# Weight buffers moved by multiples of 64 bytes against the stationary tiles of TensorE

## The chip, the cores and the metric

The kernel runs on one core of one Trainium2 chip. The metric is the device time of one execution in microseconds (us), from the program's start on the chip to its end.

## The reference

One layer of a decoder trunk, batch 1, 256 positions, 4096 channels, all in float32. A pre-RMSNorm is followed by four token mixers that share one input projection, and by a PEER channel mixer with 4096 experts:

```python
xn = rmsnorm(x, norm_mix)
cols = xn @ w_in                         # 256x4096 @ 4096x5200, split by mixer
o_a, o_b, o_c, o_d = four attention mixers of the columns
z = xn @ gate_down                       # 256 wide
merged = sum(sigmoid(z @ gate_up[i]) * (o_i @ w_branch_i) for i in range(4))
h = x + merged @ w_out                   # 4096x4096
hn = rmsnorm(h, norm_ffn)
q = hn @ peer_wq                         # 4096x1024, top-k keys and gates
out = h + (w * gelu(hn @ u.T)) @ v       # w: expert weights from the top keys
```

The weights are read once; with 256 rows, each weight tile serves two row tiles (h = 0, 1) of 128 positions.

## The kernel before, in words

**Products.** All large products run as one stream of 680 chunks. A chunk is 256 rows (two k-tiles, j = 0, 1) by up to 512 columns of weights. The activations are the stationary operand, the weights the moving one. To keep float32 accuracy with TensorE's float32r type, each operand is split in a hi and a lo part, and three products are added: hi x hi, lo x hi, hi x lo (activation x weight). One chunk is 12 matmuls: `products` (L551 on) issues 4 on L559 (activations hi, weights hi), 4 on L562 (activations lo, weights hi) and 4 on L566 (activations hi, weights lo), over j and h. `branch_products` does the same on L607, L609 and L613, `first_products` on L578, L582 and L586 for the first 16 chunks, which are 336 columns wide, `last_products` on L954 to L956 for the last chunk. The other 664 chunks are 512 columns wide: 664 x 12 = 7968 matmuls.

**Order.** The stages follow one another over the same stream: input projection (11 column groups of 16 chunks), gates and branches, output projection, PEER queries, `u` and `v`. Between chunks `between(s)` puts the small matmuls of the mixers, of the key search and of the expert scatter at slots written out by hand. Other matmuls and transposes use plain float32 or bfloat16.

**The ring.** Four slots (`RING`), each with three buffers in SBUF: `w_raw` (loaded by SP's DMA queue once `lo_ready` says that the slot's old content was split), `w_hi` (written by ACT, L979, a copy of `w_raw` into float32r, once `chunk_used` says that TensorE is done with the old chunk), and `w_lo` (DVE, L1340, `w_raw - w_hi`). TensorE waits for `hi_ready` before a chunk and for `lo_ready` before its last four matmuls. A slot's buffer is 4096 bytes in each partition: the tile of j = 0 at its start, the tile of j = 1 at `width` x 4 bytes, which is 2048 for 512 columns and 1344 for the first group's 336.

**Places.** A stationary tile is 128 columns x 4 bytes = 512 bytes in each partition. `xt_hi` and `xt_lo` begin at `XT0`, with 1024 bytes to a k-tile and h = 1 at +512; `ot_*` and `zt` are put on multiples of 512 bytes from `PJ0` by `over` (L221 on), `x2_*` begins at `PJ0` and `x3_*` at `XT0` plus whole KB. `PJ0` is a whole number of 512 bytes behind `XT0`. `w_raw`, `w_hi` and `w_lo` begin at `RG0`, at `RG0` + 16 KB and at `RG0` + 32 KB. So every 512-wide moving tile begins a whole number of 512 bytes from every stationary tile. In this document the distance of a moving tile is the remainder of that number by 512: it is 0 for all 512-wide ones, and in the first group 0 for j = 0 and 1344 - 1024 = 320 for j = 1.

**Small buffers that the diff touches.** `cmp_h` (hidden layer of the compressed keys, L709, L1054, L1450), `row_at` (a table of the key search, L1702 to L1724), `iota_h` (bfloat16 counting row, L1700, L1813, L1822), `small` (320 floats of per-row scalars, cut up by `piece`).

Of the kernel before, what the change touches and what calls it, by code (L numbers as in the profile page):

```python
# [19 lines left out]
F32R = mybir.dt.float32r  # L20
BF16 = mybir.dt.bfloat16
# [5 lines left out]
P = 128  # L27
# [39 lines left out]

RING = 4
LEAD = RING - 1
CPG = KT // 2  # L70
GRP = D // 512
MERGE = ("b", "c", "d", "a")
MIX_K = {"b": 4, "c": 4, "d": 2, "a": 4}
CH_MIX = NG1 * CPG
MIX_CH, _c = {}, CH_MIX
# [3 lines left out]
CH_OUT = _c  # L79
CH_WQ = CH_OUT + GRP * CPG  # L80
CH_U = CH_WQ + 2 * CPG
CH_V = CH_U + GRP * CPG
CH_END = CH_V + GRP * CPG

# [6 lines left out]
NCMP = (S - 32) // 16 + 1  # L91
PH, PK = 8, 16
KB = 1024
# [41 lines left out]
TURN_Q, COPY_Q, SCORE_K, COPY_K = 2, 6, 6, 10  # L135
RANK_AT = CH_WQ + CPG + COPY_K + 1
SOFTMAX_AT = RANK_AT + (NT * PH // UNITS) * STEPS
PICKS_TURN = SOFTMAX_AT + 1
SCATTER_AT = PICKS_TURN + LEAD + 2
ROUND_AT = {SCATTER_AT + n + n // 11: n for n in range(ROUNDS)}  # L140
PUT_END = max(ROUND_AT) + LEAD + 1
WEIGH_AT = {max(PUT_END + 2 + q, CH_V + CPG // 2 + 3 + q - 14 if q >= 14 else 0): q for q in range(CPG)}
# [30 lines left out]
def build(nc, io):  # L173
# [1 line left out]
    base = (nc.sbuf_base + 31) // 32 * 32  # L175
    XT0 = base
    RG0 = XT0 + 64 * KB
    MG0 = RG0 + 12 * RING * KB
    CN0 = MG0 + 32 * KB

    def at(name, shape, dt, off):
        return nc.alloc_sbuf_tensor_at(name, shape, dt, offset=off)

    cursor = [CN0]

    def const(name, shape, dt=F32):
        t = at(name, shape, dt, cursor[0])
        cursor[0] += (int(np.prod(shape[1:])) * 4 + 31) // 32 * 32
        assert cursor[0] <= nc.sbuf_usable_end, name
        return t  # L190
# [3 lines left out]
    xt_lo = at("xt_lo", [P, KT, S], F32R, XT0 + 32 * KB)  # L194

    w_raw = at("w_raw", [P, RING, 1024], F32, RG0)
    w_hi = at("w_hi", [P, RING, 1024], F32R, RG0 + 4 * RING * KB)
    w_lo = at("w_lo", [P, RING, 1024], F32R, RG0 + 8 * RING * KB)

    xt_raw = at("xt_raw", [P, KT, S], F32, MG0)  # L200
    rows = at("rows", [P, NT, D], F32, MG0)
    feat = {"c": at("feat_c", [P, 6, S], F32, MG0), "b": at("feat_b", [P, 7, S], F32, MG0 + 8 * KB),
            "d": at("feat_d", [P, 8, S], F32, MG0 + 8 * KB), "a": at("feat_a", [P, 8, S], F32, XT0),
            "i": at("idx_t", [P, 3, S], F32, MG0 + 16 * KB)}
    probs_of = [at(f"probs{h}", [P, 6, (h + 1) * P], F32, MG0 + 16 * KB) for h in range(NT)]
# [38 lines left out]
    pe_t = const("pe_t", [P, 2, 32])  # L244
    cmp_w2 = const("cmp_w2", [P, 2, P])
    cmp_b = const("cmp_b", [P, 2, 32, NCMP])
    cmp_h = const("cmp_h", [P, 2, NCMP])

    def cmp_at(i):

# [37 lines left out]
    pair_n = const("pair_n", [P, UNITS, PK], U32)  # L288
    pair_m = const("pair_m", [P, UNITS, PK], U32)
    pair_f = const("pair_f", [P, 2, UNITS, PK])  # L290
    row_at = const("row_at", [P, PK])
    fifteen = const("fifteen", [P, UNITS, PK], U32)
    iotas = const("iotas", [P, P])
    iota_h = const("iota_h", [P, P], BF16)

    square = at("square", [P, D], F32, XT0)
    peer_q = at("peer_q", [P, NT, PH * HD], F32, XT0)
# [26 lines left out]
    def piece(n, parts=P):  # L324
        used[0] += n
        return small[0:parts, used[0] - n:used[0]]
# [5 lines left out]
    row_max, row_neg, row_den, row_inv = piece(6), piece(6), piece(6), piece(6)  # L332
    nsa_gate, top8, k_ms, k_rstd = piece(24), piece(8), piece(1, NCMP), piece(1, NCMP)
    soft_den, soft_inv = piece(16), piece(16)


    acc = nc.alloc_psum_tensor("acc", [P, 2, NT, 512], F32)
# [100 lines left out]
    def mix_end(b, n):  # L438

        return MIX_CH[b] + (n + 1) * (1 + MIX_K[b] // 2) - 1  # L440


    MIX_OUT = {mix_end(b, n) + LEAD: (b, n) for b in MERGE for n in range(GRP)}
    GATE_OUT = {MIX_CH[b] + n * (1 + MIX_K[b] // 2) + LEAD: (b, n) for b in MERGE for n in range(GRP)}
    OUT_OUT = {CH_OUT + (n + 1) * CPG + LEAD: n for n in range(GRP)}

    MIX_BLOCK = {mix_end("a", n) + LEAD + 1: n for n in range(GRP)}
    MIX_STORE = {mix_end("a", n) + LEAD + 5 + i: (n, (2 * i, 2 * i + 1)) for n in range(GRP) for i in range(2)}
# [1656 lines left out]
```

How the kernel before makes its waits and increments, by code:

```python
        def then(instruction):  # L393
            count[0] += 1
            instruction.then_inc(own, 1)
            eng.wait_ge(own, count[0])
# [28 lines left out]
    def evacuated(eng, group):  # L425
        eng.wait_ge(bank_free[group % 2], group // 2 + 1)
        if group:
            eng.wait_ge(bank_free[(group - 1) % 2], (group - 1) // 2 + 1)
# [33 lines left out]
        @block.sync  # L463
# [1 line left out]
            def load(src, slot, width, used_by=None):  # L465
                if used_by is not None:
                    sp.wait_ge(lo_ready, used_by)
                sp.dma_start(w_raw[:, slot, 0:width], src).then_inc(raw_loaded[slot], 16)
# [12 lines left out]
            def load_in(chunk, g, slot, used_by=None):  # L481
                if used_by is not None:
                    sp.wait_ge(lo_ready, used_by)
                into = w_raw[:, slot, 0:2 * in_width(g)].rearrange("p (j n) -> p j n", j=2)
                end = FIRST + SKEW * g
                if g:
                    sp.dma_start(into[:, :, 0:512 - end], in_tile(chunk - CPG, slice(end - SKEW, W1C)))\
                        .then_inc(raw_loaded[slot], 16)
                sp.dma_start(into[:, :, in_width(g) - end:], in_tile(chunk, slice(0, end)))\
                    .then_inc(raw_loaded[slot], 16)
# [14 lines left out]
                        load_in(m * RING + c, g, c, m * RING + (c - RING + 1))  # L506
                if g == 6:
                    sp.wait_ge(cmp_hidden, 4)
                    sp.dma_start(dil[:], io["dil"]).then_inc(dil_loaded, 16)
```

## Time and profile before

| | us |
|---|---|
| median of the runs (2 runs, 1931.16 to 1931.26) | 1931.21 |
| the profiled execution | 1931.49 |
| its span, first to last instruction | 1929.3 |

The profiled execution lies 0.28 us above the median, and 2.2 us of it lie outside the span. In the profile, PE is the row of matmuls and PEld that of the loads of stationary tiles (LDWEIGHTS), which overlap the matmuls. The recorded length of a matmul (390 ns for 512 columns) includes its pipeline, so successive ones overlap. The pace of the stream is read from starts: the start of one group of 4 less that of the one before, over 4.

### The profile page before, as it was taken

To read this page: it belongs to the slowest core of one execution; us is meant where nothing else is said; L and a number is where in the kernel's file an instruction comes from. 1 tells how busy PE (TensorE), PEld (TensorE's weight loads), DVE (VectorE), ACT (ScalarE), POOL (GpSimd) and SP (SyncE) were. 2 spreads that over 40 slices of the span, in tenths; PEclk is the share of its full clock that TensorE was granted. 3 is DMA by queue.
4 is the path that set the end of the run, shared out by engine and by line. 5 is a ranking of instruction groups with operands and counts; after the bars stand their busy time and mean duration, and the time that the engine had idled before them with its cause. 6 is when DMAs were issued, how large, how long until landed. Compare 5 with 4: busy or idle time off the path is not lost.

```text
span 1929.3 us, 26583 instructions
## 1 busy us (share of the span) xinstructions
PE 1924.4 (100%) x9284; PEld 1588.5 (82%) x9284; DVE 1274.3 (66%) x1876; ACT 933.7 (48%) x1146; POOL 37.0 (2%) x50
## 2 busy tenths in 40 slices
PE   9999999999999999999999999999999999999999
PEld 8888888888888888888888888888887788888887
DVE  6578775675557889655555555788878876444444
ACT  6653644444566556444444464444444454333332
POOL 0010010000000000000000000000000000000000
PEclk9999999999999999999999999999999999999999
DMA  9976666566655669877777776667766578666664
GB/s 321 351 221 166 171 177 192 163 164 173 184 177 179 178 206 290 286 228 244 239 233 217 217 226 223 227 213 215 221 214 189 176 232 285 202 206 207 200 204 140
DMA packets 198537, 412.62 MB, mean 214 GB/s; under 512 B 45760, under 2 KB 123968, under 8 KB 197792
## 3 DMA queue, kind: packets, MB, share of 16 engines
q1 hardware_dynamic: 173616, 368.83, 62.9%
q10 hardware_dynamic: 20976, 25.19, 3.9%
q0 software_dynamic: 3840, 17.17, 2.4%
q8 instruction: 70, 1.15, 0.2%
q14 instruction: 35, 0.29, 0.0%
HBM read 390.15 MB, written 20.97 MB: 213 GB/s over the span
## 4 chain that ended last, share of the span: by engine, by line
PE 99%; DMA 0%; SPq 0%; ACT 0%; DVE 0%; issue 0%
PE acc L559 29%; PE acc L562 29%; PE acc L566 29%; PE acc L607 3%; PE acc L609 3%; PE acc L613 3%; PE side L737 1%; PE side L848 1%; PE acc L578 0%; PE acc L582 0%; PE acc L586 0%; PE side L772 0%; PE side L663 0%; DMA w_raw<-in_w_in 0%; PE side L748 0%; PE side L702 0%
## 5 line engine op out<-in xcount | busy, mean ns | idle before, releaser
L1340 DVE TENSOR_TENSOR w_lo<-w_raw,w_hi 128x1024 fp32r<-128x1024 f32 (+1 forms) x680 | 825.4, 1216 | 607.4 <-ACT w_hi L979 604.6
L979 ACT ACTIVATE w_hi<-w_raw 128x1024 fp32r<-128x1024 f32 (+1 forms) x680 | 715.0, 1053 | 817.8 <-PE acc L566 738.7
L559 PE MATMUL acc<-w_hi,xt_hi 128*128 128x512 f32 x1660 | 449.3, 393 | 0.0
L562 PE MATMUL acc<-w_hi,xt_lo 128*128 128x512 f32 x1660 | 444.4, 390 | 0.0
L566 PE MATMUL acc<-w_lo,xt_hi 128*128 128x512 f32 x1660 | 444.2, 390 | 0.0
L562 PEld LDWEIGHTS acc<-w_hi,xt_lo 128*128 128x128 f32 x1660 | 311.8, 188 | 65.2
L566 PEld LDWEIGHTS acc<-w_lo,xt_hi 128*128 128x128 f32 x1660 | 311.8, 188 | 64.9
L559 PEld LDWEIGHTS acc<-w_hi,xt_hi 128*128 128x128 f32 x1660 | 308.9, 188 | 63.4 <-issue 1.8
L559 PE MATMUL acc<-w_hi,x_hi 128*128 128x512 f32 x640 | 175.2, 396 | 0.0
L562 PE MATMUL acc<-w_hi,x_lo 128*128 128x512 f32 x640 | 171.9, 391 | 0.0
L566 PE MATMUL acc<-w_lo,x_hi 128*128 128x512 f32 x640 | 171.3, 390 | 0.0
L562 PEld LDWEIGHTS acc<-w_hi,x_lo 128*128 128x128 f32 x640 | 120.2, 188 | 25.6
L566 PEld LDWEIGHTS acc<-w_lo,x_hi 128*128 128x128 f32 x640 | 120.2, 188 | 25.3
L559 PEld LDWEIGHTS acc<-w_hi,x_hi 128*128 128x128 f32 x640 | 117.3, 188 | 22.4
L1121 ACT ACTIVATE gate<-acc 128x512 f32<-128x512 f32 x64 | 34.8, 596 | 35.1 <-PE acc L566 35.0
L559 PE MATMUL acc<-w_hi,zt_hi 128*128 128x512 f32 x128 | 34.5, 392 | 0.0
L566 PE MATMUL acc<-w_lo,zt_hi 128*128 128x512 f32 x128 | 34.3, 390 | 0.0
L562 PE MATMUL acc<-w_hi,zt_lo 128*128 128x512 f32 x128 | 34.3, 390 | 0.0
L1585 DVE TENSOR_TENSOR gate<-acc,gate 128x512 f32<-128x512 f32 x48 | 30.8, 683 | 0.0
L1063 ACT ACTIVATE probs<-probs,small 128x128 f32<-128x128 f32 (+2 forms) x44 | 18.3, 417 | 22.0 <-DVE small L1498 21.9
L562 PEld LDWEIGHTS acc<-w_hi,zt_lo 128*128 128x128 f32 x128 | 24.1, 188 | 5.0
L566 PEld LDWEIGHTS acc<-w_lo,zt_hi 128*128 128x128 f32 x128 | 24.0, 188 | 5.0
(279 smaller groups left out, 1345.4 us busy)
## 6 DMA issues: line engine op xcount, KB each, us to landing
w_raw<-in_stream SPq DMA_DIRECT2D x504, 512.0 KB, 4.2
w_raw<-in_w_in SPq DMA_DIRECT2D x16, 496.0 KB, 4.2
w_raw<-in_w_in SPq DMA_DIRECT2D x16, 480.0 KB, 4.0
w_raw<-in_w_in SPq DMA_DIRECT2D x16, 464.0 KB, 3.7
w_raw<-in_w_in SPq DMA_DIRECT2D x16, 448.0 KB, 3.8
w_raw<-in_w_in SPq DMA_DIRECT2D x16, 432.0 KB, 3.9
w_raw<-in_w_in SPq DMA_DIRECT2D x16, 416.0 KB, 3.9
w_raw<-in_w_in SPq DMA_DIRECT2D x16, 400.0 KB, 3.7
```

Source lines behind the costliest of these rows:

```text
L559: pe.matmul(o[h], lhs(k0 + j, h)[0], wh[j], start=first and j == 0, stop=False)
L562: pe.matmul(o[h], lhs(k0 + j, h)[1], wh[j], start=False, stop=False)
L566: mm = pe.matmul(o[h], lhs(k0 + j, h)[0], wl[j], start=False, stop=last and j == 1)
L607: pe.matmul(o, lhs(k0 + j, h)[0], wh[j], start=first and j == 0, stop=False)
L609: pe.matmul(o, lhs(k0 + j, h)[1], wh[j], start=False, stop=False)
L613: mm = pe.matmul(o, lhs(k0 + j, h)[0], wl[j], start=False, stop=last and j == 1)
L737: mm = pe.matmul(side[:, r // 2, (r % 2) * S:(r % 2) * S + nk], f[:, q, tile_rows(h)], key[:, 0:nk], start=True, stop=True)
L848: pe.matmul(side[:, n % 2, t * 64:(t + 1) * 64], hot_c[n % 3][:, t, :], flat(hot_q[:, n % 3, t, 0:2]), start=True, stop=False)
L979: nc.scalar.activation(w_hi[:, slot, 0:width], w_raw[:, slot, 0:width], ACT.Copy).then_inc(hi_ready, 1)
L1121: e = nc.scalar.activation(gate[:, n % 2, h, :], acc[:, 1, h, :], ACT.Sigmoid)
L1340: nc.vector.tensor_tensor(w_lo[:, slot, 0:width], w_raw[:, slot, 0:width], w_hi[:, slot, 0:width].bitcast(F32), ALU.subtract).then_inc(lo_ ...
L1585: nc.vector.tensor_tensor(dst, acc[:, 0, h, :], gate[:, n % 2, h, :], ALU.mult)\
```

## The change

Each slot of `w_hi` and `w_lo` becomes 64 bytes longer (`STEP` = 16 floats), and so 64 bytes more lie between the buffers of successive slots; `w_lo` begins 256 bytes later, behind the longer `w_hi`. The distances become 0, 64, 128 and 192 for `w_hi` of slots 0 to 3, and 256, 320, 384 and 448 for `w_lo`; in the first group's j = 1 tiles 320 is added to these (modulo 512). What follows the ring (`MG0` and all behind it) moves by 512 bytes and so keeps its distance. To make room, `cmp_h` and `row_at` move into unused places of `small`, and `iota_h` takes only its own 256 bytes at the end. `w_raw` and the instructions stay as they are.

```diff
--- before.py
+++ after.py
@@ -67,6 +67,7 @@
 
 RING = 4
 LEAD = RING - 1
+STEP = 16
 CPG = KT // 2
 GRP = D // 512
 MERGE = ("b", "c", "d", "a")
@@ -175,7 +176,7 @@
     base = (nc.sbuf_base + 31) // 32 * 32
     XT0 = base
     RG0 = XT0 + 64 * KB
-    MG0 = RG0 + 12 * RING * KB
+    MG0 = RG0 + 12 * RING * KB + 8 * STEP * RING
     CN0 = MG0 + 32 * KB
 
     def at(name, shape, dt, off):
@@ -194,8 +195,8 @@
     xt_lo = at("xt_lo", [P, KT, S], F32R, XT0 + 32 * KB)
 
     w_raw = at("w_raw", [P, RING, 1024], F32, RG0)
-    w_hi = at("w_hi", [P, RING, 1024], F32R, RG0 + 4 * RING * KB)
-    w_lo = at("w_lo", [P, RING, 1024], F32R, RG0 + 8 * RING * KB)
+    w_hi = at("w_hi", [P, RING, 1024 + STEP], F32R, RG0 + 4 * RING * KB)
+    w_lo = at("w_lo", [P, RING, 1024 + STEP], F32R, RG0 + 8 * RING * KB + 4 * STEP * RING)
 
     xt_raw = at("xt_raw", [P, KT, S], F32, MG0)
     rows = at("rows", [P, NT, D], F32, MG0)
@@ -244,7 +245,6 @@
     pe_t = const("pe_t", [P, 2, 32])
     cmp_w2 = const("cmp_w2", [P, 2, P])
     cmp_b = const("cmp_b", [P, 2, 32, NCMP])
-    cmp_h = const("cmp_h", [P, 2, NCMP])
 
     def cmp_at(i):
 
@@ -288,10 +288,9 @@
     pair_n = const("pair_n", [P, UNITS, PK], U32)
     pair_m = const("pair_m", [P, UNITS, PK], U32)
     pair_f = const("pair_f", [P, 2, UNITS, PK])
-    row_at = const("row_at", [P, PK])
     fifteen = const("fifteen", [P, UNITS, PK], U32)
     iotas = const("iotas", [P, P])
-    iota_h = const("iota_h", [P, P], BF16)
+    iota_h = at("iota_h", [P, P], BF16, cursor[0])
 
     square = at("square", [P, D], F32, XT0)
     peer_q = at("peer_q", [P, NT, PH * HD], F32, XT0)
@@ -332,6 +331,8 @@
     row_max, row_neg, row_den, row_inv = piece(6), piece(6), piece(6), piece(6)
     nsa_gate, top8, k_ms, k_rstd = piece(24), piece(8), piece(1, NCMP), piece(1, NCMP)
     soft_den, soft_inv = piece(16), piece(16)
+    row_at = piece(PK)
+    cmp_h = piece(2 * NCMP).rearrange("p (w n) -> p w n", n=NCMP)
 
 
     acc = nc.alloc_psum_tensor("acc", [P, 2, NT, 512], F32)
```

## Rows read from the trace of the kernel before

**Rows 1.** Page, part 1: busy us (share of span) and instructions of each engine.
```profile
PE 1924.4 (100%) x9284; PEld 1588.5 (82%) x9284; DVE 1274.3 (66%) x1876; ACT 933.7 (48%) x1146; POOL 37.0 (2%) x50
```

**Rows 2.** Page, part 4: the chain of work that ended last, by engine and line.
```profile
PE 99%; DMA 0%; SPq 0%; ACT 0%; DVE 0%; issue 0%
PE acc L559 29%; PE acc L562 29%; PE acc L566 29%; PE acc L607 3%; PE acc L609 3%; PE acc L613 3%; PE side L737 1%; PE side L848 1%; PE acc L578 0%; PE acc L582 0%; PE acc L586 0%; PE side L772 0%; PE side L663 0%; DMA w_raw<-in_w_in 0%; PE
```

**Rows 3.** Page, part 2: granted TensorE clock in 40 slices.
```profile
PEclk9999999999999999999999999999999999999999
```

**Rows 4.** Page, part 5: out<-in, shapes, count, busy us, mean ns, idle before.
```profile
L1340 DVE TENSOR_TENSOR w_lo<-w_raw,w_hi 128x1024 fp32r<-128x1024 f32 (+1 forms) x680 | 825.4, 1216 | 607.4 <-ACT w_hi L979 604.6
L979 ACT ACTIVATE w_hi<-w_raw 128x1024 fp32r<-128x1024 f32 (+1 forms) x680 | 715.0, 1053 | 817.8 <-PE acc L566 738.7
L559 PE MATMUL acc<-w_hi,xt_hi 128*128 128x512 f32 x1660 | 449.3, 393 | 0.0
```

**Rows 5.** Timeline, all engines, around 1101 us: start us, us, instruction, xcount.
```profile
1100.78 1.07 PE L559 MATMUL acc<-w_hi,xt_hi 128*128 128x512 f32 x4
1100.78 0.64 PEld L559 LDWEIGHTS acc<-w_hi,xt_hi 128*128 128x128 f32 x3
...
1101.04 1.06 ACT L979 ACTIVATE w_hi<-w_raw 128x1024 fp32r<-128x1024 f32 x1 [1.66 <-PE acc L566]
1101.46 0.87 PEld L562 LDWEIGHTS acc<-w_hi,xt_lo 128*128 128x128 f32 x4
1101.68 1.07 PE L562 MATMUL acc<-w_hi,xt_lo 128*128 128x512 f32 x4
1102.13 1.23 DVE L1340 TENSOR_TENSOR w_lo<-w_raw,w_hi 128x1024 fp32r<-128x1024 f32 x1 [1.49 <-ACT w_hi L979]
...
1102.59 1.07 PE L566 MATMUL acc<-w_lo,xt_hi 128*128 128x512 f32 x4
...
1103.50 1.07 PE L559 MATMUL acc<-w_hi,xt_hi 128*128 128x512 f32 x4
```

**Rows 6.** Timeline, PE, first group of columns (336 wide).
```profile
17.50 0.77 PE L586 MATMUL acc<-w_lo,xt_hi 128*128 128x336 f32 x4
...
23.00 0.32 PE L586 MATMUL acc<-w_lo,xt_hi 128*128 128x336 f32 x1
```

**Rows 7.** Timeline, PE, plain float32 matmuls at 400 us.
```profile
400.44 1.88 PE L772 MATMUL side<-probs_t,proj 128*128 128x512 f32 x4
402.15 1.89 PE L737 MATMUL side<-feat_c 128*128 128x256 f32 x8
```

**Rows 8.** Timeline, PE, expert scatter stage.
```profile
1500.96 1.17 PE L559 MATMUL acc<-w_hi,x_hi 128*128 128x512 f32 x4
1501.96 1.09 PE L562 MATMUL acc<-w_hi,x_lo 128*128 128x512 f32 x4
1502.89 1.07 PE L566 MATMUL acc<-w_lo,x_hi 128*128 128x512 f32 x4
1503.81 0.20 PE L848 MATMUL side<-hot_q,hot_c 128*128 128x64 bf16 x1
```

**Rows 9.** Groups of DVE by line and shape, columns as in Rows 4.
```profile
L1340 DVE TENSOR_TENSOR w_lo<-w_raw,w_hi 128x1024 fp32r<-128x1024 f32 x664 | 811.7, 1224 | 603.9 <-ACT w_hi L979 601.1
...
L1599 DVE TENSOR_TENSOR rows<-rows,gate 128x1024 f32<-128x1024 f32 x16 | 19.6, 1226 | 0.6
...
L1340 DVE TENSOR_TENSOR w_lo<-w_raw,w_hi 128x672 fp32r<-128x672 f32 x16 | 13.7, 856 | 3.5 <-ACT w_hi L979 3.4
```

**Rows 10.** Windows: stretch, length, busy us (xcount) by engine, clock, DMA share, GB/s.
```profile
1130.00:1500.00 370.00, 370.00 (x1904) 304.64 (x1903) 292.40 (x719) 166.92 (x184) 2.46 (x5) 1.00 0.69 216
```

**Rows 11.** Windows: line 1340 alone, columns as in Rows 10.
```profile
1130.00:1500.00 370.00, 159.92 (x131) 1.00 0.69 216
```

**Rows 12.** Line 1340 (DVE): durations min/median/max ns, first and last start us.
```profile
L1340 DVE TENSOR_TENSOR w_lo<-w_raw,w_hi x680: 850/1226/1230, 5.9 to 1916.4; 128x1024 fp32r<-128x1024 f32 x166, 128x672 fp32r<-128x672 f32 x4
```

## The prediction

> **What bounds the kernel now.** I read the page's busy times first, then the chain that ended last, then the clock, then the timeline. PE is busy for 1924.4 of 1929.3 us [rows 1], 99% of the chain that ended last is PE, and nearly all of it stands on the product lines L559, L562, L566 and their twins L607, L609, L613 [rows 2]; the clock is granted in full in every slice, 2.4 GHz [rows 3]. So neither loads nor ACT nor DVE bound the kernel, but the pace at which matmuls follow one another, and an edit that only moves addresses can pay in two ways alone: by that pace, or by making ACT or DVE so slow that PE waits.
>
> The pace stands in the timeline. In one chunk L559 starts at 1100.78 us and the next chunk's L559 at 1103.50 [rows 5]: 2.72 us for 12 matmuls, 226.7 ns for one. 512 columns at 2.4 GHz are 213.3 ns, so 13.4 ns of each matmul are no column. The chunk holds no wait: its three groups start 0.90, 0.91 and 0.91 us apart. What happens beside the matmul: the loads of L562's stationary tiles start at 1101.46 us, when the fourth L559 matmul starts (1100.78 + 3 x 0.227), so each matmul reads its moving tile while the next stationary tile is read [rows 5]. All of these tiles stand at distance 0. That is where a conflict of the two reads could be, and it would be worth 7968 x 13.4 ns = 107 us.
>
> Plain float32 matmuls give the floor to which such a stall could fall. Four of L772, 512 columns wide, take 402.15 - 400.44 = 1.71 us, 427.5 ns for one [rows 7]; a column takes two cycles there, 426.7 ns in all, and the load beside it costs under 1 ns. [...]
>
> **The change part by part.**
>
> *Distances.* w_hi serves 8 of the 12 matmuls of a chunk, w_lo 4. Only w_hi of slot 0 stays at distance 0: 8/12 x 1/4 = 1/6 of the matmuls. So 5/6 of 7968, 6640 matmuls, are moved, to 64 to 448. One of these distances is in the trace already: in the first group the j = 1 tiles stand at 320, half of the matmuls, with j = 0 at distance 0 beside them. There three chunks run from 17.50 to 23.00 us [rows 6]: 5.50 us over 36 matmuls, 152.8 ns for one. 336 columns are 140.0 ns, so 12.8 ns are lost for one. Had distance 320 no loss (1 ns, as plain float32), the mean loss would be (13.4 + 1)/2 = 7.2 ns, and three chunks would take 36 x 147.2 ns = 5.30 us, 0.20 us less than the 5.50 seen; at a reading error of 0.01 us for each start this is not near. Had 320 a doubled loss, they would take 36 x 160.1 = 5.76 us; nor is it that. Two starts read to 0.01 us leave 0.3 ns for one matmul, and the mean loss lies 0.6 below 13.4, so distance 320 may save between 0.6 and 1.8 ns of its own, or the narrower tile may have another price. Bounds from both sides: at best all moved matmuls fall to the float32 loss, 6640 x 12.4 ns = 82 us less; at worst they lose as much again, 6640 x 13.4 = 89 us more. I take the row that has one of the distances, and of its possible saving a small part: 0.2 ns on 6640 matmuls, 1 us. A saving of 1.2 ns on all would be 8 us.
>
> The trace speaks against an effect in another way too: h = 0 and h = 1 stand 512 bytes apart, j = 0 and j = 1 2048, the slots 4096, hi and lo 16 KB. Yet the groups of four start 0.90 to 0.91 us apart whether they read xt_hi or xt_lo, w_hi or w_lo [rows 5]. Any rule by address must thus repeat within 512 bytes. A stationary tile fills just 512 bytes, and while it is read the moving read runs through all places of such a period; a shift of its start then changes when they meet and not how often. That is argued, not seen.
>
> A rule on this stands beside the row of 226.7 ns [rows 5]. The Trainium skill, TensorE: Matmul & The Clock Gate (section "Step-by-step: what each phase is for"), says that TensorE has two independent SBUF read ports and that loading the next stationary tile takes nothing from the running matmul; its section "Back-to-back issue gap" gives 512/2.4 + 2.5 = 215.8 ns for an isolated stream. By the ports alone the change is worth nothing, as I forecast; by its gap the loss here would be 2.5 ns and not 13.4. The trace disagrees with the second by 10.9 ns, so something the page doesn't count takes time beside the load, and that keeps the first rival alive.
>
> *ACT and DVE.* ACT writes w_hi and DVE reads w_raw with w_hi and writes w_lo. Before, the three lie at distance 0 of each other; after, 64 to 448 apart. Durations: 1053 ns and 1216 ns on average, with 817.8 and 607.4 us idle before them [rows 4]. DVE's time goes by width alone: 856 ns for 672 elements and 1224 for 1024 [rows 9], (1224 - 856)/352 = 1.05 ns for one, and another subtraction-like pass with other operands, L1599, takes 1226 for 1024. The longest of all 680 is 1230 [rows 12]. I take 0; each way 0.1 us per chunk is hidden. The cover: w_hi is ready 1101.04 + 1.06 = 1102.10, w_lo at 1103.36 [rows 5], and this is work for a later chunk. It is gone where DVE is fullest, 292.4 of 370 us [rows 10]: 77.6 us over the 131 subtractions there [rows 11] is 0.59 us for one, so a subtraction must grow by half before it costs.
>
> *The small buffers.* cmp_h, row_at and iota_h are read and written by the same instructions at another address; none is on a line that the chain names [rows 2]. 0. No instruction, wait, load or queue entry is added, removed or reordered, so nothing is queued behind anything new, and the loads of w_raw keep their places.
>
> Sum: the profiled execution of 1931.5 less 1 us and nothing else is 1930.5; it stands 0.3 above the median of 1931.2, so in the median 1930.
>
> **The rivals.**
>
> *The distance frees the stall (faster).* The 13.4 ns are two reads meeting because they start at the same place. For it: they are paid only where a full-rate stream runs beside a load, and plain float32 doesn't pay them [rows 5, 7]. Against it: 320 pays almost the same [rows 6]. It would have to hold at the other distances and not at 320. In full it gives 1931 - 82 = 1849 us; if it frees half of the moved matmuls, 41 us less, 1890.
>
> *Distance 0 is the good place (slower).* A moving tile at a whole number of 512 bytes fills four blocks of 512; any other start makes it touch five, and meet the stationary read twice. Its price: from 5.8 ns, the difference between the slowest regular group in the trace, 1502.89 - 1501.96 = 0.93 us for four matmuls, 232.5 ns each [rows 8], and 226.7, up to a second 13.4 ns. 6640 x 5.8 = 39 us gives 1970; 6640 x 13.4 gives 2020. It decides for "slower by over 2%" from 5.8 ns on. Against it: the first group's j = 1 tiles, narrower though, show no such addition.
>
> *DVE's subtraction grows (slower, by another engine).* Reads of w_raw and w_hi at unequal places could take longer. It costs from +0.59 us for one subtraction; at +1.2 us it is 0.6 us for 131 chunks in the fullest stretch, 80 us, 2010. Nothing in the durations hints at it [rows 9, 12].
>
> *The distances act, but little.* The saving of 1.2 ns at 320 is real and alike elsewhere: 1931 - 8 = 1923; the opposite sign 1939. This lies inside the likeliest case.
>
> **How the numbers follow.** A difference of 2%, 39 us, is about what a measurement of this kernel can tell from no change. No change within 2%: 0.70, with its own range 1921 to 1939. Stall freed: 0.21, of which 0.19 goes beyond 2%. Distance 0 the good place: 0.08, DVE: 0.01; of both together 0.09 beyond 2%. The part of the freed stall that stays within 2% makes that case 0.72. Predicted is 1930 us. The range must hold 8 in 10: 1865 to 1950 leaves out the fullest part of the first rival (about 0.1) and the second's (about 0.09).
>
> **What would show it.** Right: a chunk still takes 2.72 us in the timeline, PE's share stays at 99% to 100%, L1340 and L979 keep their means of 1216 and 1053 ns, and the first group's three chunks 5.50 us. Since each slot has its own distances, an effect would show as groups of four of unequal length by slot: with the first rival fully true, L566's group (w_lo) falls from 0.91 to 0.86 us in all slots, L559's and L562's in three of four. I am wrong if a group's spacing moves by more than 0.02 us, or if PE idles before L559 or L566.

## The result, and the profile after

The changed kernel takes 1963.62 us (median of 2 runs, 1963.53 to 1963.70) against 1931.21 us: ratio 1.0167, 95% interval 1.0147 to 1.0188. It is slower by 32.4 us. That is 1.7%, still inside the 2% that the prediction called no change (0.72), but outside the stated range (1865 to 1950), beyond its upper end, where the prediction left about 0.09.

The page of the changed kernel: span, busy times of the engines, granted clock, the chain that ended last, and the costliest groups (busy us, mean ns, idle before). The inserted line moves line numbers by one.

```profile
span 1961.4 us, 26583 instructions
...
PE 1956.9 (100%) x9284; PEld 1590.5 (81%) x9284; DVE 1275.5 (65%) x1876; ACT 933.1 (48%) x1146; POOL 37.1 (2%) x50
...
PEclk9999999999999999999999999999999999999999
...
PE 100%; DVE 0%; issue 0%
PE acc L560 29%; PE acc L567 29%; PE acc L563 29%; PE acc L608 3%; PE acc L610 3%; PE acc L614 3%; PE side L738 1%; PE acc L579 1%; PE side L849 1%; PE acc L583 1%; PE acc L587 1%; PE side L773 0%; PE side L664 0%; PE side L594 0%; PE side 
...
L1341 DVE TENSOR_TENSOR w_lo<-w_raw,w_hi 128x1024 fp32r<-128x1024 f32 (+1 forms) x680 | 825.9, 1216 | 636.9 <-ACT w_hi L980 633.5
L980 ACT ACTIVATE w_hi<-w_raw 128x1024 fp32r<-128x1024 f32 (+1 forms) x680 | 715.0, 1052 | 853.7 <-PE acc L567 782.8
L560 PE MATMUL acc<-w_hi,xt_hi 128*128 128x512 f32 x1660 | 458.1, 398 | 0.0
L567 PE MATMUL acc<-w_lo,xt_hi 128*128 128x512 f32 x1660 | 450.4, 393 | 0.0
```

Against [rows 1 to 4]: the clock is still granted in full, the chain is still PE alone, and ACT's copy (1053 ns before, 1052 now) and DVE's subtraction (1216 ns) last as long as before. Both idle more, 853.7 for 817.8 us and 636.9 for 607.4: they wait for a TensorE that got slower. The product lines carry the difference.

Four successive chunks in the timeline of PE of the changed kernel (start us, us, instruction, count); they sit in slots 1, 2, 3 and 0:

```profile
1104.83 1.10 PE L560 MATMUL acc<-w_hi,xt_hi 128*128 128x512 f32 x4
1105.77 1.07 PE L563 MATMUL acc<-w_hi,xt_lo 128*128 128x512 f32 x4
1106.68 1.08 PE L567 MATMUL acc<-w_lo,xt_hi 128*128 128x512 f32 x4
1107.60 1.10 PE L560 MATMUL acc<-w_hi,xt_hi 128*128 128x512 f32 x4
1108.53 1.09 PE L563 MATMUL acc<-w_hi,xt_lo 128*128 128x512 f32 x4
1109.45 1.10 PE L567 MATMUL acc<-w_lo,xt_hi 128*128 128x512 f32 x4
1110.39 1.09 PE L560 MATMUL acc<-w_hi,xt_hi 128*128 128x512 f32 x4
1111.32 1.09 PE L563 MATMUL acc<-w_hi,xt_lo 128*128 128x512 f32 x4
1112.25 1.09 PE L567 MATMUL acc<-w_lo,xt_hi 128*128 128x512 f32 x4
1113.18 1.09 PE L560 MATMUL acc<-w_hi,xt_hi 128*128 128x512 f32 x4
1114.11 1.07 PE L563 MATMUL acc<-w_hi,xt_lo 128*128 128x512 f32 x4
1115.02 1.07 PE L567 MATMUL acc<-w_lo,xt_hi 128*128 128x512 f32 x4
1115.92 0.40 PE L560 MATMUL acc<-w_hi,xt_hi 128*128 128x512 f32 x1
```

The pace is the difference of starts. [rows 5] have 2.72 us for a chunk; here slot 1 takes 1107.60 - 1104.83 = 2.77, slots 2 and 3 2.79 each, and slot 0 2.74. Slot 0's last group, with w_lo at distance 256, takes 0.90 us as before, and all groups of slot 3 (w_hi at 192, w_lo at 448) take 0.93. No group waits for anything. But a group's pace doesn't follow its own distance alone: slot 0's first group, at distance 0, takes 0.93 us, and slot 1's first, at 64, takes 0.94 where its other two take 0.91 and 0.92. The run with slot 3's w_hi at 192 takes this up.

Summed from start to start over the whole trace, the 512-wide chunk matmuls take 1819.3 us before and 1851.1 after, the 336-wide ones 30.2 and 30.2, and all others 75.0 and 75.2. So 31.8 of the 32.1 us by which the span grew lie in the 512-wide chunk matmuls, 4.0 ns for each on average.

### The profile page after: what moved, and what is told of

Read it like the earlier page. It is cut to its first block, busy times and chain, and to the rows that moved or that the text cites. A ratio compares the mean times of both kernels' runs of the same rounds, so it can differ in the third digit from the quotient of the medians.

```text
span 1961.4 us, 26583 instructions
## 1 busy us (share of the span) xinstructions
PE 1956.9 (100%) x9284; PEld 1590.5 (81%) x9284; DVE 1275.5 (65%) x1876; ACT 933.1 (48%) x1146; POOL 37.1 (2%) x50
## 4 chain that ended last, share of the span: by engine, by line
PE 100%; DVE 0%; issue 0%
PE acc L560 29%; PE acc L567 29%; PE acc L563 29%; PE acc L608 3%; PE acc L610 3%; PE acc L614 3%; PE side L738 1%; PE acc L579 1%; PE side L849 1%; PE acc L583 1%; PE acc L587 1%; PE side L773 0%; PE side L664 0%; PE side L594 0%; PE side L749 0%; PE side L703 0%
## 5 line engine op out<-in xcount | busy, mean ns | idle before, releaser
L1341 DVE TENSOR_TENSOR w_lo<-w_raw,w_hi 128x1024 fp32r<-128x1024 f32 (+1 forms) x680 | 825.9, 1216 | 636.9 <-ACT w_hi L980 633.5
L980 ACT ACTIVATE w_hi<-w_raw 128x1024 fp32r<-128x1024 f32 (+1 forms) x680 | 715.0, 1052 | 853.7 <-PE acc L567 782.8
L560 PE MATMUL acc<-w_hi,xt_hi 128*128 128x512 f32 x1660 | 458.1, 398 | 0.0
L567 PE MATMUL acc<-w_lo,xt_hi 128*128 128x512 f32 x1660 | 450.4, 393 | 0.0
L563 PE MATMUL acc<-w_hi,xt_lo 128*128 128x512 f32 x1660 | 449.5, 392 | 0.0
```

Source lines behind the costliest of these rows:

```text
L560: pe.matmul(o[h], lhs(k0 + j, h)[0], wh[j], start=first and j == 0, stop=False)
L563: pe.matmul(o[h], lhs(k0 + j, h)[1], wh[j], start=False, stop=False)
L567: mm = pe.matmul(o[h], lhs(k0 + j, h)[0], wl[j], start=False, stop=last and j == 1)
L980: nc.scalar.activation(w_hi[:, slot, 0:width], w_raw[:, slot, 0:width], ACT.Copy).then_inc(hi_ready, 1)
L1341: nc.vector.tensor_tensor(w_lo[:, slot, 0:width], w_raw[:, slot, 0:width], w_hi[:, slot, 0:width].bitcast(F32), ALU.subtract).then_inc(lo_ ...
```

## The experiments

All kernels below have the reference's arithmetic. Unless said otherwise they hold the change's moves of the small buffers and its 512 bytes of room behind the ring, and put the ring elsewhere:

```diff
-    MG0 = RG0 + 12 * RING * KB
+    MG0 = RG0 + 12 * RING * KB + 512
```

Each was run once, beside a run of the kernel before on the same chip; those runs lie between 1931.06 and 1931.31 us. "Pace" is the mean from start to start over the 512-wide chunk matmuls that another chunk matmul follows, gaps over 260 ns left out, worked out from the starts in each trace. The kernel before has 227.1 ns by this count. Matmuls of a chunk are counted from 0.

**All at 192.**

```diff
-    w_raw = at("w_raw", [P, RING, 1024], F32, RG0)
-    w_hi = at("w_hi", [P, RING, 1024], F32R, RG0 + 4 * RING * KB)
-    w_lo = at("w_lo", [P, RING, 1024], F32R, RG0 + 8 * RING * KB)
+    w_raw = at("w_raw", [P, RING, 1024], F32, RG0 + 192)
+    w_hi = at("w_hi", [P, RING, 1024], F32R, RG0 + 4 * RING * KB + 192)
+    w_lo = at("w_lo", [P, RING, 1024], F32R, RG0 + 8 * RING * KB + 192)
```

> All three buffers of the ring (w_raw, w_hi, w_lo) begin 192 bytes later, so every 512-wide moving tile stands at distance 192 and the buffers stand to each other as before. Theory A (the distance between moving and stationary tile sets the pace; in the changed kernel slot 3 holds 192 and 448 and shows 233.3 ns a matmul): a chunk takes 12 x 233.3 = 2.80 us, the kernel 1931 + 7968 x 6.6 ns = 1984 us. Theory B (what ACT and DVE read and write at unequal places of the ring disturbs TensorE's read of the ring): 1931 us, 2.72 us a chunk.

Measured: 1979.93 us. Timeline of PE of this kernel, one chunk:

```profile
1102.24 1.10 PE L559 MATMUL acc<-w_hi,xt_hi 128*128 128x512 f32 x4
1103.17 1.09 PE L562 MATMUL acc<-w_hi,xt_lo 128*128 128x512 f32 x4
1104.11 1.10 PE L566 MATMUL acc<-w_lo,xt_hi 128*128 128x512 f32 x4
1105.04 1.10 PE L559 MATMUL acc<-w_hi,xt_hi 128*128 128x512 f32 x4
```

2.80 us for the chunk, 0.93 and 0.94 for each group of four; the pace is 233.3 ns, and as a mean over the trace it lies between 233.0 and 233.6 at every one of the 12 places in every slot. Single matmuls are not that even: in this chunk they take 231 and 235 or 236 ns in turn, and in the last stage (from 1616 us) the places alternate between 235.8 and 230.8. The kernel's time is theory A's to 4 us; theory B, which expected no change, fails.

**All at 64.** The same edit with 64.

> The same with 64 bytes for all three buffers. Theory A: the changed kernel's groups at 64 and 320 take about 228.5 ns a matmul, so 1931 + 7968 x 1.8 ns = 1945 us (1940 to 1960), the same length of chunk in every slot. Theory B: 1931 us.

Measured: 1947.18 us, pace 229.0 ns, equal in all slots. That is 2 us from theory A and 16 from theory B.

**Only w_raw at 192.**

```diff
-    w_raw = at("w_raw", [P, RING, 1024], F32, RG0)
-    w_hi = at("w_hi", [P, RING, 1024], F32R, RG0 + 4 * RING * KB)
-    w_lo = at("w_lo", [P, RING, 1024], F32R, RG0 + 8 * RING * KB)
+    w_raw = at("w_raw", [P, RING, 1024], F32, RG0 + 192)
+    w_hi = at("w_hi", [P, RING, 1024], F32R, RG0 + 4 * RING * KB + 512)
+    w_lo = at("w_lo", [P, RING, 1024], F32R, RG0 + 8 * RING * KB + 512)
```

> w_raw begins 192 bytes later, w_hi and w_lo 512, so the moving tiles keep distance 0 and only ACT's and DVE's read of w_raw stands at 192 from what they write. Theory A: 1931 us. Theory B: slower, at least the 3 us a 19 ns rise per chunk in one slot of four would make, up to the 32 us of the change.

Measured: 1931.06 us. Timeline of PE, the starts of two successive chunks:

```profile
1103.05 1.07 PE L559 MATMUL acc<-w_hi,xt_hi 128*128 128x512 f32 x4
...
1105.77 1.07 PE L559 MATMUL acc<-w_hi,xt_hi 128*128 128x512 f32 x4
```

2.72 us, as before. Unequal places of w_raw and of what ACT and DVE make from it cost nothing.

**Only slot 3's w_hi at 192.** Slots become tensors of their own, so that one can stand apart:

```diff
+    class Slots:
+        def __init__(self, name, dt, places):
+            self.t = [at(f"{name}{i}", [P, 1024], dt, p) for i, p in enumerate(places)]
+        def __getitem__(self, key):
+            return self.t[key[1]][:, key[2]]
...
-    w_hi = at("w_hi", [P, RING, 1024], F32R, RG0 + 4 * RING * KB)
-    w_lo = at("w_lo", [P, RING, 1024], F32R, RG0 + 8 * RING * KB)
+    w_hi = Slots("w_hi", F32R, [RG0 + (4 * RING + 4 * i) * KB + d for i, d in enumerate((0, 0, 0, 192))])
+    w_lo = Slots("w_lo", F32R, [RG0 + (8 * RING + 4 * i) * KB + d for i, d in enumerate((512, 512, 512, 512))])
```

> Only w_hi of slot 3 stands at 192; w_hi of slots 0 to 2 and all of w_lo at 0. In the changed kernel the first group of four matmuls of slot 0 takes 230.8 ns each although its own distance is 0, while ACT writes w_hi of slot 3 at 192. Theory A alone: slot 3's w_hi groups at 233.3, all others 226.7 to 227.3: 1931 + 8 x 166 x 6.6 ns = 1940 us. Theory A with an addition by ACT's write: slot 0's first group also rises to about 231, 3 us more, 1943 us.

Measured: 1942.02 us, between the two sums. Timeline of PE; the chunk of slot 3 starts at 1098.27 us, that of slot 0 at 1101.06, that of slot 1 at 1103.78:

```profile
1098.27 1.09 PE L568 MATMUL acc<-w_hi,xt_hi 128*128 128x512 f32 x4
1099.20 1.09 PE L571 MATMUL acc<-w_hi,xt_lo 128*128 128x512 f32 x4
1100.14 1.08 PE L575 MATMUL acc<-w_lo,xt_hi 128*128 128x512 f32 x4
1101.06 1.07 PE L568 MATMUL acc<-w_hi,xt_hi 128*128 128x512 f32 x4
1101.97 1.07 PE L571 MATMUL acc<-w_hi,xt_lo 128*128 128x512 f32 x4
...
1103.78 1.07 PE L568 MATMUL acc<-w_hi,xt_hi 128*128 128x512 f32 x4
```

The two w_hi groups of slot 3 take 0.93 and 0.94 us. The third, whose distance is 0, takes 0.92, where 0.91 is its pace elsewhere. Place by place, mean ns from start to start over the trace:

```
slot 3, matmuls 6 to 11:  233.3 233.3 | 226.7 235.1 228.9 232.3
slot 0, matmuls 0 to 5:   230.3 227.3 228.0 227.5 227.1 227.4
slot 1, matmuls 0 to 5:   226.7 227.3 227.5 227.1 227.0 227.4
```

The fall from 192 to 0 is not at once: the first matmul at 0 takes 226.7 ns, as it would in the kernel before, the second takes the longest of all, and the series fades over five or six. It begins inside slot 3's own chunk, so it isn't ACT's write of slot 3's buffer, as I had offered for slot 0's high first group in the changed kernel: that group comes behind slot 3's w_lo at 448, and shows the same series from its first matmul on, 226.7, 234.8, 229.5, 231.8 and 230.1 ns. The additions over 226.7 sum to 8.4 + 2.2 + 5.6 + 3.6 = about 20 ns for each fall.

**All at 128.** The same edit as all at 192, with 128.

> The whole ring 128 bytes later. Runs so far: 226.9 ns a matmul at distance 0, 229.0 at 64, 233.3 at 192. If the pace rises evenly from 64 to 192, 128 gives about 231 ns: 1931 + 7968 x 4.2 ns = 1965 us. If what counts is only how far a tile is from the nearest multiple of 256, 128 is the worst place, over 233.3: above 1980 us.

Measured: 1974.67 us, pace 232.5 ns: neither the even rise (231) nor the worst place.

**All at 256.**

> The whole ring 256 bytes later. Theory A with a period of 256 bytes (the changed kernel's slot 0 has w_lo at 256 and shows 226.9 ns): 1931 us, 226.9 ns. With a period of 512 bytes only: some other pace in all slots, and 1940 us or more.

Measured: 1931.60 us, pace 227.1 ns. 256 is as good as 0. It also serves as the control for the small buffers: their move costs at most 0.5 us.

**Everything 192 later.** No room is added behind the ring here.

```diff
-    XT0 = base
+    XT0 = base + 192
```

> All buffers, stationary ones and the ring, begin 192 bytes later: the distance stays 0, the places themselves move. Theory A (distance): 1931 us. Rival C (the place of the moving tile itself, by its remainder of 256 or 512, sets the pace, whatever the stationary tile's): 233.3 ns a matmul and 1980 us as in the run with the ring alone 192 later.

Measured: 1931.41 us. Timeline of PE, the starts of two successive chunks:

```profile
1100.70 1.07 PE L559 MATMUL acc<-w_hi,xt_hi 128*128 128x512 f32 x4
...
1103.42 1.07 PE L559 MATMUL acc<-w_hi,xt_hi 128*128 128x512 f32 x4
```

2.72 us. With the ring alone 192 later a chunk takes 2.80; with the stationary tiles 192 later as well, 2.72. So for 512-wide tiles the place of the moving tile is not what counts: it is the distance. Rival C falls.

**All at 32.**

> The whole ring 32 bytes later. If the pace follows the distance evenly near 0, 32 gives between 226.9 and 229.0 ns, about 228: 1931 + 9 = 1940 us. If 0 is no best place, 32 falls below 226.9 ns and the kernel below 1925 us.

Measured: 1980.57 us, pace 233.3 ns. Both expectations fall: 32 bytes cost as much as 192, and more than 64.

**Only the stationary buffer xt_lo moved, by 192 and by 64.** The ring stands at 256 in both.

```diff
-    xt_lo = at("xt_lo", [P, KT, S], F32R, XT0 + 32 * KB)
+    xt_lo = at("xt_lo", [P, KT, S], F32R, XT0 + 32 * KB + 192)
```

> The ring stands 256 bytes later (distance 0) and only the stationary buffer xt_lo 192 bytes later, so that in chunks with xt_lo only its four stationary tiles of twelve are off. If a matmul's pace is set by its moving tile and the NEXT stationary tile, which is loaded while it runs, matmuls 4 to 7 of a chunk (the last of L559 and the first three of L562) take longer. If it is its OWN stationary tile, matmuls 5 to 8 (all of L562). Either way 4 x 6.6 ns and a slow return as after slot 3's w_hi in the earlier run (about 20 ns) make 46 ns for each of the 415 chunks that use xt_lo: 1931 + 19 = 1950 us.

> Ring 256 bytes later (distance 0), xt_lo alone 64 bytes later: against xt_lo the moving tiles stand at 192, where the pace is a flat 233.3 ns. A drop from 192 to 0 shows as 226.7, 235.1, 228.9, 232.3, 230.3 ns (the run with slot 3's w_hi at 192), the rise is at once. Moving tile against NEXT stationary tile: matmuls 3 to 6 of a chunk (counted from 0) take 233.3 ns, matmul 7 226.7, matmul 8 235.1. Moving tile against its OWN stationary tile: 4 to 7 take 233.3, 8 226.7, 9 235.1. The kernel 1931 + 415 x (26 + 20) ns = 1950 us either way.

Measured: 1942.50 us with 192 and 1952.32 with 64. I had left out in the first expectation that a stationary tile 192 later makes the distance -192, which is 64 by the remainder of 256, the cheaper place. Timeline of PE with xt_lo 64 later, one chunk:

```profile
1852.43 1.08 PE L559 MATMUL acc<-w_hi,xt_hi 128*128 128x512 f32 x4
1853.35 1.09 PE L562 MATMUL acc<-w_hi,xt_lo 128*128 128x512 f32 x4
1854.28 1.09 PE L566 MATMUL acc<-w_lo,xt_hi 128*128 128x512 f32 x4
1855.20 1.08 PE L559 MATMUL acc<-w_hi,xt_hi 128*128 128x512 f32 x4
```

0.92, 0.93 and 0.92 us with 0.91 before. Place by place in the last stage, matmuls 0 to 11, mean of all slots:

```
xt_lo 192 later: 226.7 226.1 227.0 226.1 229.1 231.2 226.1 236.1 228.4 231.9 231.1 226.9
xt_lo  64 later: 232.5 230.3 227.0 226.0 235.8 230.3 236.1 229.4 230.8 230.3 236.2 228.6
before:          226.6 226.3 227.1 226.6 226.5 226.8 226.7 226.4 226.9 226.5 226.5 227.0
```

Only chunks with xt_lo got slower: by 10.6 us in sum with 192 and 20.7 with 64, while those with x_lo, zt_lo and ot_lo keep their sums to 0.1 us. So a stationary tile that moves costs as a moving one does. The series fits neither of the two clean patterns that were expected: four flat places at 233.3 don't show. But the places aren't flat in the run with all at 192 either; in the last stage they alternate between 235.8 and 230.8 there, and places 4 to 7 with xt_lo 64 later (235.8, 230.3, 236.1, 229.4) look like that. These are the matmuls whose own stationary tile moved. Matmul 3 takes 226.0 and 226.1 ns, no longer than before, although the first moved tile is loaded beside it (the loads of L562 start at 1853.12 us, when that matmul does). That speaks against the tile loaded beside the matmul as the simple partner; what follows place 7 fits neither pattern, and the question stays open.

**Surveys of the distances between.** Slots at 96, 160, 224 and 256, and slots at 16, 48, 80 and 112 (the views start 4 floats into tensors that lie 32 bytes further apart from slot to slot), w_lo at the same remainders of 256:

```diff
+    ... enumerate((96, 160, 224, 256))
...
+    ... first + (4 * KB + 32) * i) ... key[2].start + 4:key[2].stop + 4
```

> Slots 0 to 3 stand at 96, 160, 224 and 256, w_lo at the same remainders of 256, so 12 matmuls run at each distance. If 64 (229.0 ns) is one dip in a plateau, 96, 160 and 224 take 232 to 234 ns and the kernel (3/4 x 6.3 ns + 5 ns for the return to 0 spread over 12) x 7968 = 1931 + 40 to 50 us. If a place better than 0 exists, one slot settles below 226.6 ns.

> Slots 0 to 3 at distances 16, 48, 80 and 112 (w_lo at the same remainders of 256). If 0 is the best place because both streams then start in step, all four lie above 227.0 ns; 48, 80 and 112 at 229 to 234 ns and the kernel at 1960 to 1980 us. If a small offset beats 0, slot 0 settles below 226.6 ns.

Measured: 1975.36 and 1966.71 us. The last group of four of each slot: 234.2 ns at 96, 233.7 at 160, 233.3 at 224, 226.8 at 256, and 231.8 at 16, 233.2 at 48, 230.6 at 80, 229.6 at 112. In the second run each slot still carries something of the one before, so its numbers are rough. As expected, 160 and 224 lie between 232 and 234 ns, 96 just above, and both kernels in their ranges (1971 to 1981, 1960 to 1980). No distance tried has a shorter pace than 0 and 256, and so none of the runs beats the kernel before; I know of no version that does.

The paces of the runs in which all slots stand alike, from the traces:

| distance | pace, ns | kernel, us |
|---|---|---|
| 0 (before) | 227.1 | 1931.2 |
| 32 | 233.3 | 1980.6 |
| 64 | 229.0 | 1947.2 |
| 128 | 232.5 | 1974.7 |
| 192 | 233.3 | 1979.9 |
| 256 | 227.1 | 1931.6 |

These put the change together. Its w_hi stands at 0, 64, 128 and 192 and its w_lo at the same four by the remainder of 256. The mean of the four kernels is (1931.2 + 1947.2 + 1974.7 + 1979.9)/4 = 1958.2 us. The changed kernel's 1963.6 lies 5.4 us above: that is what going from one distance to another adds, 5.4 us over 166 rounds of the ring, 32 ns for a round. Slot by slot, the changed kernel's places have a mean of 228.5, 230.3, 232.7 and 233.0 ns, against 227.1, 229.0, 232.5 and 233.3 in the table: 2.7 ns more in sum, 32 ns over 12 matmuls, and nearly all of it in slots 0 and 1.

## Why the prediction was wrong

**What held.** TensorE's pace is the bound, and the change could act by it or not at all. ACT, DVE and the small buffers cost nothing: 1216 ns and 1052 ns as before, and 1931.1 us with w_raw moved alone. A matmul's loss depends on addresses by a period of at most 512 bytes; for 512 columns the runs give 256.

**The step that failed: "Distances".** This term stood in the sum as 1 us less (0.2 ns saved on each of 6640 moved matmuls); it measured 32.4 us more, 4.9 ns for each. I valued distance 320 from the first group, where j = 1 stands at 320, and took it over to 512-wide tiles and to all other distances. The row was read rightly, and it speaks for 336 columns only. Timelines of PE in the first group, three chunks from the first row to the second, first with all at 32 (j = 0 at 32, j = 1 at 352, which is 96 by the remainder of 256), then with all at 128 (128 and 192), last with everything 192 later, where the distances are those of the kernel before:

```profile
17.84 0.78 PE L586 MATMUL acc<-w_lo,xt_hi 128*128 128x336 f32 x4
...
23.36 0.78 PE L586 MATMUL acc<-w_lo,xt_hi 128*128 128x336 f32 x4
```

```profile
16.69 0.78 PE L578 MATMUL acc<-w_hi,xt_hi 128*128 128x336 f32 x4
...
22.29 0.78 PE L578 MATMUL acc<-w_hi,xt_hi 128*128 128x336 f32 x4
```

```profile
17.48 0.77 PE L586 MATMUL acc<-w_lo,xt_hi 128*128 128x336 f32 x4
...
22.99 0.78 PE L586 MATMUL acc<-w_lo,xt_hi 128*128 128x336 f32 x4
```

5.52, 5.60 and 5.51 us over 36 matmuls, 153.3, 155.6 and 153.1 ns, against 152.8 before [rows 6]. Narrow tiles thus take some tenths of a ns more with unchanged distances too (from all starts of chunks 4 to 15: 152.5 before, 153.3 with everything 192 later, and 153.3 with all at 32). So nothing of the 0.5 ns at 32 can be put down to the distance; the 2.8 at 128 stand out. 512-wide matmuls pay 6.2 at 32 and about 7 at 96, 5.4 at 128 and 6.2 at 192. The narrow tiles pay from next to nothing to a half of it, so their row was weak evidence for the wide ones, and the prediction names that doubt in half a sentence ("or the narrower tile may have another price") and gives it no weight in the chances. 320 is by the period of 256 the place 64, which is besides the cheapest of those tried apart from 0: 1.9 ns at full width, against 5.4 and 6.2 at 128 and 192. So even a right value for 320 would not have held for the others.

**The argument that failed with it.** "A shift of its start then changes when they meet and not how often." The period was inferred rightly from equal groups; that nothing follows from a shift inside the period was a thought that no row bore, and the prediction says so itself; the runs refute it: 32 bytes cost 6.2 ns for each matmul.

**The rivals.** The one on the other side, distance 0 as the good place, came true in sign and nearly in size: 5.8 ns for 6640 moved matmuls, 39 us, was its lower end; measured are 32.4 us, 4.9 ns for one. Its mechanism did not: a tile at 256 touches five blocks of 512 bytes as one at 192 does and pays nothing. The 5.8 ns came from a group of the kernel before that stands at distance 0 [rows 8], so that the size came near is luck. The range ended at 1950 because its chance was set at 0.08. The first rival, a stall freed by the distance, shows nowhere: no distance tried is faster than 0. The prediction also took 39 us for about what a measurement can tell from no change; here all executions of the kernel before lie between 1931.06 and 1931.49 us. Its own sign of being wrong, a group's spacing moved by more than 0.02 us, did come: 0.94 for 0.90 us in slot 1.

The Trainium skill, TensorE: Matmul & The Clock Gate (section "Step-by-step: what each phase is for"), says that loading the next stationary tile takes nothing from the running matmul. The runs bear that out in part only. Matmul 3 is no longer while the first moved tile of xt_lo is loaded beside it (226.0 ns). But with the same instructions the distance between stationary and moving tiles sets the pace of 512-wide float32r matmuls between 227.1 and 233.3 ns, and xt_lo moved alone by 64 bytes costs 21 us. So where a stationary tile stands is not free for the matmuls around its load, and there the measurement decides; which of them pays isn't shown.

**Still open.** Why a remainder of 256 bytes, why 64 is cheap between 32 and 128, what the 13.4 ns at distance 0 are, whether the load of the next stationary tile is the partner, why 336 columns pay so much less, and what costs them 0.8 ns when everything moves by 192 bytes. Widths between 336 and 512 were not tried.

## What to carry to other kernels

Where float32r matmuls of 512 columns run back to back, each with a new stationary tile, keep stationary and moving tiles a whole number of 256 bytes apart, and pad rings and buffers in whole 256 bytes; 32 stray bytes cost 2.6% of this kernel. Read the pace of matmuls from starts, place by place in the chunk and slot by slot, since a busy share of 100% shows nothing of it. A row of another width is evidence for that width: give what it can't show a chance of its own before the range is closed.

## What was not expected of the hardware

The pace doesn't follow the distance evenly: 227.1 ns at 0, 233.3 at 32, 229.0 at 64, 232.5 at 128, 233.3 at 192, 227.1 at 256. It isn't even from matmul to matmul: with all at 192 it alternates between about 231 and 236 ns in the last stage. And it has a memory: after a fall from 192 to 0 the matmuls take 226.7, 235.1, 228.9, 232.3 and 230.3 ns before they settle, about 20 ns for each such step, so a mix of distances costs more than the mean of its parts.
